# One key group's maximum subtracted on GpSimd, and a first tile stored from a copy, in a transformer block on one core

## The chip, the cores and the metric

The kernel runs on one core of a Trainium2 chip. The metric is device time of one execution in microseconds, the median of several runs. Five engines work side by side and are tied by semaphores only: TensorE (PE), VectorE (DVE), ScalarE (ACT), GpSimd (POOL) and SyncE (SP), which here issues the DMAs.

## The reference, cut to what matters

A block of a diffusion transformer over 2048 tokens and 256 context tokens of width 1024: modulated norm, projections, latent attention with 8 heads, a two-way retention with 8 heads, an output projection and a layer of 16 experts. The change touches the attention and the first tile of the projection.

```python
def block_attention(q, k, v):
    ...
    def one_block(qblk):
        s = jnp.einsum('bqhd,bkhd->bhqk', qblk, k).astype(jnp.float32) * scale
        p = jax.nn.softmax(s, axis=-1).astype(v.dtype)
        return jnp.einsum('bhqk,bkhd->bqhd', p, v)
...
    h = rmsnorm(x, g_norm_mix[layer]) * (1.0 + sc1) + sh1
    hc = rmsnorm(ctx, g_norm_mix[layer]) * (1.0 + csc1) + csh1
```

Each head has queries of width 96, 2048 of them, and 2304 keys. All is float32.

## The kernel before

The stages follow one another: projection (`project`), retention, attention (`attention`), output projection, experts.

**Attention** (lines 1220 to 1562) takes 32 blocks `b`, each one head and 512 queries. The keys are 18 tiles of 128 (`T`), in six groups of three (`GROUPS`, `G`). A block's scores stand with keys on the partitions and queries along the row, in one of two SBUF tiles `sc` of 18 x 512; blocks take them in turn. Every engine runs `turn(pair, j, b, more)` for each block; the order inside is written by hand, and an engine does its instructions in that order.

- TensorE (L1413): the scores of block b+1, tile by tile through four PSUM banks, each as three matmuls (`score`, L1368). After tile 11 come the probability sums of block b-1 (`prob_sum`, L1409), which need all of GpSimd's sums. Tile 12 may only overwrite its bank when VectorE's held maximum has read it. Then the weighted sum of block b in six groups (`weighted`, L1399). After group 2 it transposes the maxima of block b+1 (`max_rows`, L1380), after group 3 it spreads the column maxima over all partitions (`max_spread`, L1388: a matmul of a repeated column with the identity), into PSUM bank 4.
- ScalarE (L1470): exponential of group 0 (`probabilities`, L1462), nine score copies of b+1 out of PSUM (`copy_scores`, L1457), exponential of group 1, nine more copies, exponentials of groups 2 to 4, the finished output of b-1 (L1468), a part of the rounding of the next head's keys and queries (L1450), exponential of group 5.
- VectorE (L1547): subtraction of the maximum in groups 2 to 5 of block b (`shift`, L1545, which reads the spread maximum from PSUM); then the maximum over the keys of b+1: the held maximum (L1511) takes tiles 0, 1 from SBUF and 8, 9 from their PSUM banks, once tile 9 has been copied; six more pairs (L1518), the fold (L1525 to L1528), column maxima (`spread`, L1539), and the subtraction in groups 0 and 1 of b+1.
- GpSimd (L1343): a part of the splitting of the next head's keys and queries in six of eight blocks (`split`, L1341, two instructions), then five sums of the probabilities over the groups (L1349 once, L1353 four times), each after its exponential.
- SyncE stores each finished block and loads heads.

For the last block TensorE waits for GpSimd's sums and adds them (L1442).

**Projection.** For each of 18 token tiles VectorE makes `h_T_whole` (modulate, L649, L651), ScalarE rounds it (L547), VectorE forms the rest (`rest`, L659), and TensorE multiplies by the input weights (`z`, L410). The unrounded tile lies where the rest is written, so `rest` first waits until it is stored (`h_stored`). For tile 0 the store is issued by ScalarE (L604), for later ones by SyncE. ScalarE also rounds two parts of the input weights (L596) ahead of the statistics of tile 1. `kz` (`k_zeta`) is GpSimd's output of L616, first written in tile 0 after the retention keys are ready.

## Time and profile before

| | |
|---|---|
| median of 3 runs | 2913.35 us (2909.04 to 2915.96) |
| profiled execution | 2910.62 us, span 2908.8 us |
| busy over the span | PE 2607.9 us (90%), DVE 1975.1 (68%), ACT 1466.8 (50%), POOL 977.0 (34%) |
| 1100 to 1700 us, within attention | PE 536.89 of 600 us, DVE 486.45, ACT 456.85, POOL 450.29 |
| the same, granted TensorE clock | 1.00 |

Busy time tells how full an engine is, not what it waits for. For that the rows further down go through one block in order of time. In a timeline a row is a run of like instructions: start, time to its end, engine, line, operation, output<-input, shapes, count; in square brackets the idle time before it, and who ended it. Matmul ends are modelled, so the next start is the better mark of what a run costs. A float32 matmul is recorded as two or more instructions.

### The profile page before, as it was taken

The page shows a single profiled execution, that of the slowest core. Times are in us where ns is not written, and L with a number is a line of the kernel's source. Part 1 is how long each engine was busy: PE and PEld are TensorE (multiplying, and loading weights), DVE is VectorE, ACT ScalarE, POOL GpSimd, SP SyncE. Part 2 cuts the span into 40 slices and gives each one's busy share as a digit, 9 for nine tenths or more (in the row PEclk, how much of TensorE's full clock was granted, in tenths as well). Part 3 has the DMA queues.
Part 4 walks back from the last instruction along what each step waited for, and adds up shares of the span by engine and source line. Part 5 has one row for each costly group of instructions (what it writes and reads, how often), then busy time and mean ns, then how long its engine had stood idle before and what let it go on. Part 6 is the DMA issues. An engine that isn't in the chain of part 4 may idle for free. (4 is left out here: it accounts for less than half of the span.)

```text
span 2908.8 us, 44417 instructions
## 1 busy us (share of the span) xinstructions
PE 2607.9 (90%) x17109; PEld 2170.1 (75%) x17109; DVE 1975.1 (68%) x2885; ACT 1466.8 (50%) x2178; POOL 977.0 (34%) x578
## 2 busy tenths in 40 slices
PE   5999999899959898989889949992999999999996
PEld 3877877788846666666666628881999999999995
DVE  5555554777748887888788835557766767767666
ACT  4555554322237777877777732112344444444444
POOL 0111111222216777777777652220101101101112
PEclk7999999999969999999999979995999999999998
DMA  7644443322230110111010035434667767767678
GB/s 254 206 153 153 154 163 131 98 79 79 64 63 3 37 38 14 28 37 29 15 36 6 7 103 169 154 129 139 190 205 229 220 203 229 232 202 228 208 231 304
DMA packets 278856, 379.67 MB, mean 131 GB/s; under 512 B 36755, under 2 KB 200502, under 8 KB 276982
## 3 DMA queue, kind: packets, MB, share of 16 engines
q1 hardware_dynamic: 268998, 341.70, 36.9%
q0 software_dynamic: 9504, 34.61, 5.2%
q8 instruction: 137, 2.24, 0.3%
q14 instruction: 73, 0.60, 0.1%
q10 hardware_dynamic: 144, 0.52, 0.0%
HBM read 290.87 MB, written 85.90 MB: 130 GB/s over the span
## 5 line engine op out<-in xcount | busy, mean ns | idle before, releaser
L2143 PE MATMUL ebank<-gathered_T,w_gate_up 128*128 128x256 f32 x4608 | 546.5, 280 | 1.4 <-DVE gathered_T L2365 1.4
L2143 PEld LDWEIGHTS ebank<-gathered_T,w_gate_up 128*128 128x128 f32 x4608 | 543.2, 189 | 3.2 <-DVE gathered_T L2365 1.8
L1353 POOL TENSOR_TENSOR prob_sums<-prob_sums,scores 128x1536 f32<-128x1536 f32 x128 | 445.7, 3482 | 161.3 <-ACT scores L1462 147.4
L1545 DVE TENSOR_TENSOR scores<-scores,max_bank 128x1536 f32<-128x1536 f32 x192 | 322.4, 1748 | 59.3 <-PE max_bank L1388 59.3
L1462 ACT ACTIVATE scores<-scores 128x1536 f32<-128x1536 f32 x192 | 277.4, 1478 | 112.5 <-DVE scores L1545 112.5
L410 PE MATMUL bank<-w_in_sb,h_T 128*128 128x512 f32 (+1 forms) x1296 | 290.9, 383 | 12.1 <-DVE h_T L659 12.1
L1368 PE MATMUL score_banks<-head_qT,head_kT 96*128 96x512 f32 x960 | 254.3, 401 | 51.9 <-DVE max_bank L1511 33.9
L2157 PE MATMUL ebank<-w_down,hidden_T 128*128 128x512 f32 x1152 | 282.0, 400 | 3.1 <-DVE w_down L2375 2.9
L410 PEld LDWEIGHTS bank<-w_in_sb,h_T 128*128 128x128 f32 x1296 | 242.2, 189 | 46.5 <-DVE h_T L659 12.3
L1399 PE MATMUL abank<-scores,head_v 128*64 128x256 f32 x2304 | 270.3, 383 | 1.1 <-ACT scores L1462 0.9
L1368 PEld LDWEIGHTS score_banks<-head_qT,head_kT 96*128 96x128 f32 x960 | 177.6, 190 | 106.4 <-ACT scores L1457 42.6
L2076 POOL DMA_INDIRECT scratch_acc<-expert_out,slot_tokens x30 | 71.0, 2366 | 545.3 <-DVE expert_out L2394 540.8
L2157 PEld LDWEIGHTS ebank<-w_down,hidden_T 128*128 128x128 f32 x1152 | 213.8, 189 | 52.6 <-issue 4.8
L1518 DVE TENSOR_TENSOR max_bank<-scores,max_bank 128x1024 f32<-128x1024 f32 x192 | 236.0, 1229 | 20.4 <-ACT scores L1457 0.5
L1457 ACT ACTIVATE scores<-score_banks 128x512 f32<-128x512 f32 x320 | 190.7, 596 | 75.4 <-PE score_banks L1368 64.8
L1399 PEld LDWEIGHTS abank<-scores,head_v 128*64 128x64 f32 x2304 | 156.9, 137 | 91.8 <-issue 17.3
L2370 DVE TENSOR_TENSOR w_gate_up<-w_gate_up_whole,w_gate_up 128x2048 fp32r<-128x2048 f32 x96 | 215.4, 2285 | 13.5 <-ACT w_gate_up L2185 13.5
L1704 PE MATMUL obank<-w_o_sb,mix_tile 128*128 128x512 f32 x768 | 184.1, 396 | 26.8 <-POOL mix_tile L1679 26.8
L1368 PE MATMUL abank<-head_qT,head_kT 96*128 96x512 f32 x768 | 197.6, 393 | 0.0
L2185 ACT ACTIVATE w_gate_up<-w_gate_up_whole 128x2048 fp32r<-128x2048 f32 x96 | 178.2, 1905 | 37.3 <-DMA w_gate_up_whole<-in_w_exp_up 37.3
L2204 ACT ACTIVATE gate_exp<-ebank 128x256 f32<-128x256 f32 x96 | 36.8, 384 | 311.6 <-PE ebank L2143 311.6
L1704 PEld LDWEIGHTS obank<-w_o_sb,mix_tile 128*128 128x128 f32 x768 | 143.6, 190 | 56.0 <-POOL mix_tile L1679 27.2
(297 smaller groups left out, 4163.4 us busy)
## 6 DMA issues: line engine op xcount, KB each, us to landing
w_gate_up_whole<-in_w_exp_gate SPq DMA_DIRECT2D x48, 1024.0 KB, 5.9
w_gate_up_whole<-in_w_exp_up SPq DMA_DIRECT2D x48, 1024.0 KB, 8.8
w_down_whole<-in_w_exp_down SPq DMA_DIRECT2D x192, 256.0 KB, 5.8
ada_rest<-in_w_ada SPq DMA_DIRECT2D x16, 1024.0 KB
x_tile<-in_x_all SPq DMA_DIRECT2D x18, 512.0 KB
scratch_h<-h_T_whole SPq DMA_DIRECT2D x17, 512.0 KB, 2.7
ada_w<-in_w_ada SPq DMA_DIRECT2D x4, 2048.0 KB, 19.2
chunk_h_T_whole<-scratch_h SPq DMA_DIRECT2D x16, 512.0 KB
```

The source lines that it names most:

```text
L410: m = pe.matmul(banks[bank][:, 0:n], hT[u][:, hp, k, :], w_in[:, wp, k, lo:lo + n], start=(k == 0 and i == 0), stop=(k == KD - 1 and i == 2))
L1353: pool.tensor_tensor(a[:, :, :], a[:, :, :], p[:, g * G:(g + 1) * G, :], ALU.add).then_inc(sg["summed"].sem, 1)
L1368: m = pe.matmul(banks[S_BANKS[kt % 4]][:, :], kT[u][:, kp, k], qT[u][:, qp, q], start=(n == 0), stop=(n == 2))
L1399: m = pe.matmul(ps[64 * half:64 * half + 64, 0:HB], v1[u][:, kt, :], p[:, kt, half * HB:(half + 1) * HB], start=(kt == 0), stop=(kt == T - ...
L1457: act.activation(sc[j % 2][:, kt, :], banks[S_BANKS[kt % 4]][:, :], ACT.Copy).then_inc(sg["scores"].sem, 1)
L1462: act.activation(x, x, ACT.Exp, scale=ATT_SCALE).then_inc(sg["probs"].sem, 1)
L1518: dve.tensor_tensor(mx_psum[:, :, :], sc[j % 2][:, 2 * n:2 * n + 2, :], mx_psum[:, :, :], ALU.max).then_inc(sg["max_keys"].sem, 1)
L1545: dve.tensor_tensor(x, x, mid(banks[4], G), ALU.subtract).then_inc(sg["shifted"].sem, 1)
L1704: x = pe.matmul(banks[2 * u + half][:, :], mt[u][:, mp, k, :], w_o[:, wp, k, half * 512:(half + 1) * 512], start=(k == 0 and n == 0), stop ...
L2143: x = pe.matmul(banks[f % 3][:, j * CAP:(j + 1) * CAP], w_gu[c][:, wp, j, k, o:o + P], xsT[:, xp, k, :], start=(k == 0 and n == 0), stop=( ...
L2157: x = pe.matmul(banks[Y_BANKS[2 * c + h]][:, :], hid[:, hp, k, h * P:(h + 1) * P], w_d[i % RING][:, wp, :], start=(k == 0 and n == 0), sto ...
L2370: dve.tensor_tensor(w_gu[c][:, 1, j], w_gu_whole[c][:, 1, j], w_gu[c][:, 0, j].bitcast(F32), ALU.subtract).then_inc(sg["gu_rest"].sem, 1)
```

## The change

In attention, the subtraction of the maximum in group 5 (key tiles 15 to 17) goes from VectorE to GpSimd, which does it as the first instruction of its turn. GpSimd reads the maximum from a new SBUF tile `mx_all`. To fill it, TensorE spreads the maximum twice, into bank 4 and bank 3, with transposes in place of matmuls, and one key tile sooner: after two of the three tiles of group 3. ScalarE copies bank 3 to `mx_all` at the start of its turn. ScalarE copies ten score tiles, in place of nine, ahead of the exponential of group 1. In the last block GpSimd makes no sums and TensorE adds all 18 probability tiles; it takes the sums of block 30 after weighted group 0 in place of group 3. In the projection, GpSimd copies the first h tile into the still unused `kz`, and SyncE stores it from there; VectorE's `rest` of tile 0 waits for that copy and no longer for the store.

```diff
+            sp.wait_ge(h_kept, 2)
+            sp.dma_start(scratch["h"][0:P], kept).then_inc(sg["h_stored"].sem, 16)
...
-            sg["hT"].wait(act, 0)
-            act.dma_start(scratch["h"][0:P], hT_whole[0][:, 1, :, :]).then_inc(sg["h_stored"].sem, 16)
...
+                if t == 0:
+                    pool.wait_ge(h_kept, 3)
...
+            for g in range(2):
+                sg["hT"].wait(pool, 0, 2 * g + 2)
+                pool.tensor_copy(kept[:, 4 * g:4 * g + 4, :], hT_whole[0][:, 1, 4 * g:4 * g + 4, :]).then_inc(h_kept, 1)
...
-                sg["h_stored"].wait(dve, t)
+                if t:
+                    sg["h_stored"].wait(dve, t)
...
+                    if t == 0:
+                        dve.wait_ge(h_kept, g + 1)
...
             def turn(pair, j, b, more):
 
+                sg["max_kept"].wait(pool, b)
+                x = sc[j % 2][:, (GROUPS - 1) * G:, :]
+                pool.tensor_tensor(x, x, mid(mx_all[:, :], G), ALU.subtract).then_inc(sg["pool_shift"].sem, 1)
                 split_next(split, pair, j)
+                if not more:
+                    return
...
-                    m = pe.matmul(banks[4][:, c * P:(c + 1) * P], mq[:, c:c + 1].to_broadcast([P, P]), perm["ident"][:, :],
-                                  start=True, stop=True, skip_group_check=True)
+                    m = pe.transpose(banks[4][:, c * P:(c + 1) * P], mq[:, c:c + 1].to_broadcast([P, P]), perm["ident"][:, :])
                 m.then_inc(sg["max_psum"].sem, 1)
+                for c in range(4):
+                    m = pe.transpose(banks[3][:, c * P:(c + 1) * P], mq[:, c:c + 1].to_broadcast([P, P]), perm["ident"][:, :])
+                m.then_inc(sg["max_twice"].sem, 1)
...
-                    m = weighted(u, j, b, g)
-                    if more and g == 2:
+                    if more and g == 3:
                         max_rows(b + 1)
-                    if more and g == 3:
+                        weighted(u, j, b, g, range(2))
                         max_spread(b + 1)
-                    if not more and g == 3:
+                        m = weighted(u, j, b, g, range(2, G))
+                    else:
+                        m = weighted(u, j, b, g)
+                    if not more and g == 0:
                         prob_sum((j - 1) % 2, b - 1)
...
-            prob_sum((BLOCKS - 1) % 2, BLOCKS - 1)
+            ps, p = banks[5 + (BLOCKS - 1) % 2], sc[(BLOCKS - 1) % 2]
+            for kt in range(T):
+                for c in range(4):
+                    m = pe.matmul(ps[32 * c:32 * c + 32, HB:HB + P], ones[:, :], p[:, kt, c * P:(c + 1) * P],
+                                  start=False, stop=(kt == T - 1), skip_group_check=True)
+            m.then_inc(sg["out_psum"].sem, 1)
...
+            def keep_max(b):
+                sg["max_twice"].wait(act, b)
+                sg["pool_shift"].wait(act, b - 1)
+                act.activation(mx_all[:, :], banks[3], ACT.Copy).then_inc(sg["max_kept"].sem, 1)
...
             def turn(pair, j, b, more):
+                keep_max(b)
                 probabilities(j, b, 0)
                 if more:
                     sg["valued"].wait(act, b - 1)
-                    for g in range(3):
-                        copy_scores((j + 1) % 2, b + 1, g)
+                    copy_scores((j + 1) % 2, b + 1, 0, HELD + 2)
                 probabilities(j, b, 1)
                 if more:
-                    for g in range(3, GROUPS):
-                        copy_scores((j + 1) % 2, b + 1, g)
+                    copy_scores((j + 1) % 2, b + 1, HELD + 2, T)
...
-                sg["max_psum"].wait(dve, b - 1)
+                sg["max_kept"].wait(dve, b - 1)
...
-                for g in range(2, GROUPS):
+                for g in range(2, GROUPS - 1):
                     shift(j, b, g)
```

The first tile's `kz` also has to wait for its store: SyncE raises `h_kept` to 3 once the store has landed, after it has issued the store of the retention keys.

## Rows read from the trace of the kernel before

**Rows 1.** The head of the page.
```profile
span 2908.8 us, 44417 instructions
```

**Rows 2.** Waits, 874 to 1717 us: engine and line, releaser, us in total, times, longest.
```profile
DVE max_bank L1511 <- ACT scores L1457: 45.7, 31, 1.5
...
PE max_bank L1380 <- DVE score_max L1528: 50.5, 30, 2.0
...
PE score_banks L1368 <- DVE max_bank L1511: 33.9, 31, 1.9
```

**Rows 3.** Timeline of PE over one block: start, length, instructions, idle before.
```profile
1217.19 1.66 PE L1368 MATMUL score_banks<-head_qT,head_kT 96*128 96x512 f32 x6
...
1225.58 0.86 PE L1409 MATMUL abank<-prob_sums,ones 128*32 128x128 f32 x24
1227.51 1.61 PE L1368 MATMUL score_banks<-head_qT,head_kT 96*128 96x512 f32 x6 [1.07 <-DVE max_bank L1511]
...
1231.76 4.11 PE L1399 MATMUL abank<-scores,head_v 128*64 128x256 f32 x36
1237.54 0.66 PE L1380 MATMUL max_bank<-ident,score_max 128*128 128x128 f32 x4 [1.67 <-DVE score_max L1528]
1238.12 1.52 PE L1399 MATMUL abank<-scores,head_v 128*64 128x256 f32 x12
1239.57 1.16 PE L1388 MATMUL max_bank<-ident,max_cols 128*128 128x128 f32 x8
1240.66 2.81 PE L1399 MATMUL abank<-scores,head_v 128*64 128x256 f32 x24
1243.40 1.67 PE L1368 MATMUL score_banks<-head_qT,head_kT 96*128 96x512 f32 x6
```

**Rows 4.** Timeline of DVE over the same block.
```profile
1226.13 1.23 DVE L1511 TENSOR_TENSOR max_bank<-scores,score_banks 128x1024 f32<-128x1024 f32 x1 [1.50 <-ACT scores L1457]
...
1236.80 0.69 DVE L1528 TENSOR_TENSOR score_max<-score_max,max_bank 128x512 f32<-128x512 f32 x1
1238.23 0.69 DVE L1539 TENSOR_REDUCE max_cols<-max_bank 128x4 f32<-128x512 f32 x1 [0.75 <-PE max_bank L1380]
1240.77 10.07 DVE L1545 TENSOR_TENSOR scores<-scores,max_bank 128x1536 f32<-128x1536 f32 x6 [1.84 <-PE max_bank L1388]
```

**Rows 5.** Timeline of ACT over the same block.
```profile
1223.64 0.60 ACT L1457 ACTIVATE scores<-score_banks 128x512 f32<-128x512 f32 x1
1224.14 1.48 ACT L1462 ACTIVATE scores<-scores 128x1536 f32<-128x1536 f32 x1
1225.52 0.58 ACT L1457 ACTIVATE scores<-score_banks 128x512 f32<-128x512 f32 x1
```

**Rows 6.** Timeline of POOL over the same block.
```profile
1233.92 14.37 POOL L1353 TENSOR_TENSOR prob_sums<-prob_sums,scores 128x1536 f32<-128x1536 f32 x4 [4.75 <-ACT scores L1462]
```

**Rows 7.** Groups of POOL by shape: busy us, mean ns, idle before.
```profile
L1349 POOL TENSOR_TENSOR prob_sums<-scores 128x1536 f32<-128x1536 f32 x32 | 111.3, 3477 | 55.5 <-ACT scores L1462 55.5
...
L616 POOL TENSOR_TENSOR k_zeta<-ret_k_rows,zeta 128x512 f32<-128x512 f32 x36 | 44.5, 1255 | 337.6 <-DVE ret_k_rows L671 337.6
L1341 POOL TENSOR_TENSOR head_kT<-head_kT_whole,head_kT 96x768 fp32r<-96x768 f32 x21 | 39.0, 1856 | 33.4 <-ACT head_kT L1450 33.4
```

**Rows 8.** Timelines of DVE and PE at the end of attention.
```profile
1683.01 0.69 DVE L1528 TENSOR_TENSOR score_max<-score_max,max_bank 128x512 f32<-128x512 f32 x1
...
1712.20 1.51 PE L1409 MATMUL abank<-prob_sums,ones 128*32 128x128 f32 x24 [11.85 <-POOL prob_sums L1353]
```

**Rows 9.** Timelines of DVE, PE and ACT at the opening.
```profile
54.05 1.29 DVE L659 TENSOR_TENSOR h_T<-h_T_whole,h_T 128x512 fp32r<-128x512 f32 x2 [6.38 <-DMA scratch_h<-h_T_whole]
...
55.39 11.85 PE L410 MATMUL bank<-w_in_sb,h_T 128*128 128x416 f32 x48 [11.54 <-DVE h_T L659]
...
61.76 0.52 ACT L554 ACTIVATE z_latent<-bank 128x416 f32<-128x416 f32 x1 [2.26 <-PE bank L410]
```

**Rows 10.** Line 1545 alone: ns min/median/max, first and last start us.
```profile
L1545 DVE TENSOR_TENSOR scores<-scores,max_bank x192: 1744/1747/1756, 874.7 to 1695.3; 128x1536 f32<-128x1536 f32 x192
```

More of the change, by code:

```diff
@@ L216, in project @@
         zero_state = sem("zero_state")
+        h_kept = sem("first_h_kept")
+        kept = kz[:, :, :, :].rearrange("p h w d -> p (h w d)").rearrange("p (k n) -> p k n", k=KD)
         w_rounded = sem("w_in_rounded")
@@ L366, in turn @@
                 store(t, "ret_k", rk[:, :], scratch["rk"][at, :], "rk_stored")
+                if t0 == 0:
+                    sg["h_stored"].wait(sp, 0)
+                    sp.sem_inc(h_kept, 1)
                 if ahead:
@@ L1244, in attention @@
         mx = sb("score_max", [P, QB])
+        mx_all = sb("max_spread", [P, QB])
         mq = sb("max_cols", [P, 4])
@@ L1387, in max_spread, with weighted @@
                 for c in range(4):
-                    m = pe.matmul(banks[4][:, c * P:(c + 1) * P], mq[:, c:c + 1].to_broadcast([P, P]), perm["ident"][:, :],
-                                  start=True, stop=True, skip_group_check=True)
+                    m = pe.transpose(banks[4][:, c * P:(c + 1) * P], mq[:, c:c + 1].to_broadcast([P, P]), perm["ident"][:, :])
                 m.then_inc(sg["max_psum"].sem, 1)
-            def weighted(u, j, b, g):
+                for c in range(4):
+                    m = pe.transpose(banks[3][:, c * P:(c + 1) * P], mq[:, c:c + 1].to_broadcast([P, P]), perm["ident"][:, :])
+                m.then_inc(sg["max_twice"].sem, 1)
+            def weighted(u, j, b, g, part=range(G)):
                 ps, p = banks[5 + j % 2], sc[j % 2]
@@ L1396, in weighted @@
                 sg["probs"].wait(pe, b, g + 1)
-                for kt in range(g * G, (g + 1) * G):
+                for kt in (g * G + t for t in part):
                     for half in range(2):
@@ L1450, in split, with copy_scores @@
                     act.activation(x[:, 0, c], whole[:, 1, c], ACT.Copy).then_inc(sg["rounded"].sem, 1)
-            def copy_scores(j, b, g):
-                sg["summed"].wait(act, b - 2, max(g, 1))
-                for kt in range(g * G, (g + 1) * G):
+            def copy_scores(j, b, first, end):
+                for kt in range(first, end):
+                    if kt % G == 0:
+                        sg["summed"].wait(act, b - 2, max(kt // G, 1))
                     sg["s_psum"].wait(act, b, kt + 1)
                     act.activation(sc[j % 2][:, kt, :], banks[S_BANKS[kt % 4]][:, :], ACT.Copy).then_inc(sg["scores"].sem, 1)
+            def keep_max(b):
+                sg["max_twice"].wait(act, b)
+                sg["pool_shift"].wait(act, b - 1)
+                act.activation(mx_all[:, :], banks[3], ACT.Copy).then_inc(sg["max_kept"].sem, 1)
             def probabilities(j, b, g):
                 x = sc[j % 2][:, g * G:(g + 1) * G, :]
-                sg["shifted"].wait(act, b, g + 1)
+                if g < GROUPS - 1:
+                    sg["shifted"].wait(act, b, g + 1)
+                else:
+                    sg["pool_shift"].wait(act, b)
                 act.activation(x, x, ACT.Exp, scale=ATT_SCALE).then_inc(sg["probs"].sem, 1)
@@ L1492, in _ @@
                 split(0, 0, n)
-            for g in range(GROUPS):
-                copy_scores(0, 0, g)
+            copy_scores(0, 0, 0, T)
             split(1, 1, 0)
```

5 lines of the change are left out of this document (3 added, 2 removed).

## Prediction

> **What bounds the kernel now.** I read the page first: the profiled execution spans 2908.8 us [rows 1], and attention, from about 874 to 1714 us, is the only stretch that the edit reaches over and over (32 blocks). Then I read the list of waits over that stretch, then one block on each engine in order of time. The waits name two stops of TensorE that recur in every block: it waits for the held maximum (33.9 us in 31 times) and for the folded maximum (50.5 us in 30 times). The held maximum on VectorE waits in its turn for a score copy of ScalarE, 45.7 us in 31 times, 1.5 us each [rows 2].
>
> One block shows how the three hang together. Let S be the moment at which TensorE begins the scores of the next block. S is 1217.19, the next one is 1243.40, so the period is 26.21 us [rows 3]. Scores of twelve key tiles and the 24 records of the probability sums end at 1225.58 + 0.86 = S+9.25; TensorE waits 1.07 us; scores of the last six tiles run from 1227.51 to 1231.76 (4.25); three groups of the weighted sum take 4.11; it waits 1.67 us; then four transposes (0.58 to the next start), one weighted group, the spreading and two more groups, 5.86 us from 1237.54 to the next S [rows 3]. The two waits are 2.74 us; 23.47 us are work.
>
> VectorE begins the held maximum H at 1226.13 = S+8.94 and ends the fold F at 1236.80 + 0.69 = 1237.49 = H+11.36, with nothing idle between; TensorE begins the transposes 0.05 us later [rows 3, 4]. So the period is the sum (S to H) 8.94 + (H to F) 11.36 + 0.05 + 5.86 = 26.21 us. VectorE is not what delays H: its six subtractions end at 1240.77 + 10.07 = 1250.84, 1.5 us before the next H would come. H waits for the copy of key tile 9. ScalarE copies tile 8 at 1223.64, then puts the exponential of group 1 (1.48 us) in front, and copies tile 9 only at 1225.52, up to 1226.10 [rows 5].
>
> **The change in attention.** (a) The copy order. Ten tiles are now copied before the exponential of group 1. Tile 9 follows tile 8 at TensorE's pace, twelve tiles in 8.39 us or 0.70 us each [rows 3]: copy 9 runs from about 1224.34 to 1224.92, and H comes at S+7.76 instead of S+8.94, 1.18 us sooner. The exponential of group 1 then ends near S+9.1 and the copies of tiles 10 and 11 near S+10.3. They are wanted by the maximum of the sixth pair at H+5.3 = S+13, and by the scores of tile 14 at S+10.6, so this part costs nothing; the cover is 0.3 us at tile 14.
>
> (b) One subtraction of six leaves VectorE, 10.07/6 = 1.68 us. VectorE was waiting for the copy at that point, so this buys nothing by itself. It keeps (a) from running into a new wait: with six subtractions VectorE would be free at about the new S+6.4, with five at S+4.7, both before S+7.76.
>
> (c) TensorE. The held maximum ends at S+9.0 and the sums at S+9.25, so the wait of 1.07 us goes. TensorE reaches the transposes after 9.25 + 4.25 + 4.11 = S+17.61, and the fold now ends at 7.76 + 11.36 = S+19.12: what is late next is the same fold, with a wait of 1.56 us in the place of 1.67. The spreading was four plain matmuls, 8 records, 1.09 us to the next start; it becomes four transposes, whose price stands in the transposes of the maximum, 0.58 us [rows 3], and these are issued twice: 1.16, so +0.07. It also moves one key tile forward. It would start 0.58 + 0.97 (8 of 12 records of 1.45 us) after the transposes began, F+1.60; the column maxima, which it needs, are ready 1.43 us after F (1238.23 + 0.69) [rows 4]. That leaves 0.17 us of cover. VectorE can start to subtract at about F+2.3 instead of F+3.28, ScalarE's first exponential ends before the next S, and its score copies wait for TensorE, as they do now.
>
> (d) ScalarE gets one copy of 128x512 from PSUM, 0.60 us by a score copy [rows 5]. It waits for the second spreading (F+2.9) and lies ahead of the exponential of group 0, which waits for VectorE until F+4.1. It is done at F+3.5, so it is hidden. If it were not, up to 0.6 us per block would shift the exponential, which has 1.1 us before the first score copy.
>
> (e) GpSimd. It does five sums a block, four of them in 14.37 us [rows 6], 3.58 from one to the next, and two weight splits of 1.86 us in three blocks of four [rows 7]. The subtraction is not in the trace. Nearest is the two-operand add of the same shape, 3.48 us; a multiply by a repeated operand takes 1.26 us for 512 columns, which times three is 3.77 us [rows 7]. Below 3.48 I see no row; the bounds are 3.4 and 3.8 and I take 3.58 with its gap, since the shape is the same. The load of a block with splits is 6 x 3.58 + 3.7 = 25.2 us, against a new period of 25.1: just full. Without splits it is 21.5. The four adds begin when the exponential of group 2 is done, S+15.65 (now 1233.92 = S+16.73), and end at the next S+4.9; subtraction to S+8.5, splits to S+12.2, first add to S+15.7. Who waits for this: the probability sums on TensorE at S+8.4, 3.5 us of slack; the exponential of group 5 at S+20.4, 12 us of slack; ScalarE's copies into the old score tile, more. A drift of 0.1 us a block is given back in each fourth block.
>
> The new period is 7.76 + 11.36 + 0.05 + 5.86 + 0.07 = 25.10 us, 1.11 less. 31 blocks have the next block's scores beside them: 34.4 us.
>
> **The end of attention.** The fold of the last block ends at 1683.01 + 0.69 = 1683.70. Now TensorE waits 11.85 us for GpSimd's last sum and ends at 1712.20 + 1.51 = 1713.71, F+30.0 [rows 8]. In the new kernel GpSimd does no sums of block 31. It ends those of block 30 at F+10.9 (1233.92 + 14.37 stands at F+10.8 of its block [rows 4, 6]); TensorE, which now asks for them right after group 0, adds them by F+11.8, then does four weighted groups by F+17.3, the fifth by F+18.7 (GpSimd's subtraction ends at F+14.5, its exponential at F+16). Then come 72 sum matmuls in the place of 12: 6 x 0.86 = 5.2 us, F+23.8. Gain 6.2 us. TensorE stood idle for 11.85 us before its records took 1.51 instead of 0.86 us; if its clock is low after the 3.5 us stop too, up to 3.5 us are lost; if not, nothing. I take nothing and keep 3.5 for the range.
>
> **The opening.** VectorE waited 6.38 us, from 47.67 to 54.05, until the first hidden tile was stored, and TensorE began its first product at 55.39 [rows 9]. Now VectorE waits for a GpSimd copy. No row shows a GpSimd copy; by the 1.26 us of its multiply of 512 columns [rows 7] the second half is kept at 48.9 and subtracted by 49.6, so TensorE starts some 5.7 us sooner. What is late next is ScalarE: it stood 2.26 us before the latent copy at 61.76, so it is free for it at 59.50 [rows 9], held up by the weight rounding and the statistics of the next tile, which the edit doesn't move. The latent chain hence gains 2.26 us only and TensorE will wait for it. I take 2.3, with 1 and 5.5 as ends. The store goes to SyncE's queue, behind its loads and ahead of the load of the third x tile. That load is wanted some 29 us later. GpSimd's first k_zeta must wait for the store, which lands long before.
>
> **Sum.** 34.4 + 6.2 + 2.3 = 42.9 us. Against the profiled execution's 2910.62 us this gives 2867.7; that one ran 2.73 us below the median of the runs, 2913.35, so on the median 2870.4.
>
> **A rule that speaks against the move.** GpSimd and VectorE both work through the stretch, and the VectorE subtraction took 1744 to 1756 ns in all 192 cases, beside a GpSimd add or not [rows 10]. The Trainium skill, "Perfetto Trace Analysis", section Optimizing Scalar/DVE Operations, warns that offloading between VectorE and GpSimd might not help, since they share an SBUF read port. This case's trace does not bear the warning out so far for this form, whose second operand is in PSUM; rival 1 is what it would mean here.
>
> **Rivals.** (1) The two engines hold each other up after all. GpSimd's subtraction runs from S+4.9 to S+8.5; if VectorE may not start in it, H moves from S+7.76 to S+8.5 and the block gains 0.37 us: 31 x 0.37 + 8.5 = 20 us, 2893. Against it stand the even durations of rows 10. Chance 5%.
>
> (2) The held maximum does not come sooner, because the wait for the kept maximum or the copies' pace takes the place of the exponential. Then the block keeps 26.2 us and the ends alone gain 8.5: 2905. Half of it is as possible: TensorE's 0.17 us of cover is gone or tile 14 waits, 0.3 us a block, 2880; that half lies within my range. Chance of the full case 4%.
>
> (3) GpSimd becomes the bound and the kernel is slower. Mean load is 5 x 3.58 + 0.75 x 3.7 + x = 20.7 + x, so beyond x = 5.5 us for the subtraction the period exceeds the present 26.2. At twice the add, 7.0 us, it is 27.7, 1.5 us more in each of 31 blocks, +46 - 8.5 = +38 us, 2951. For it: GpSimd is full to 0.1 us in blocks with splits. Against it: rows 7 bound x by 3.8. Chance 5%.
>
> (4) More is gained: TensorE without any wait would have a period of 23.5 us, but the fold chain forbids it. The opening at its upper end and a first block that ran at the low clock could give 4 us more. That lies in the range.
>
> **How the numbers follow.** Forecast 2870, chance 84% with the small variants; rivals 5, 4, 5%, 2% for anything else. The range goes from 2860 (opening 3.2 more, noise of the runs, 0.2 us a block more) to 2886 (tail clock 3.5, opening 1.3, 0.35 us a block less). A difference under 0.2%, 5.8 us, can't be told from no change; faster by more than that 93%, within it 2%, slower 5%.
>
> **What would show it.** In the trace after: period near 25.1; no wait of TensorE for the held maximum and about 1.5 us for the fold; VectorE idle near 3 us ahead of the held maximum, still released by a score copy; GpSimd's subtraction near 3.5 us and no idle in blocks with splits; at the end a TensorE wait of 3.5 us for sums and 144 records. A period above 25.5, or a TensorE wait for prob_sums within the blocks, would prove the reckoning wrong.

## The result and the profile after

The median is 2865.11 us (4 runs, 2864.64 to 2872.16) beside 2912.84 us for the kernel before in the same job: a ratio of 0.984, 95% interval 0.982 to 0.986. The forecast was 2870 us, with a range of 2860 to 2886. The profiled execution took 2864.79 us; its head, where [rows 1] has 2908.8 us:

```profile
span 2862.8 us, 44715 instructions
...
PE 2607.9 (91%) x17229; PEld 2170.4 (76%) x17229; DVE 1921.4 (67%) x2853; ACT 1490.4 (52%) x2210; POOL 1072.7 (37%) x607
```

TensorE is busy for the same 2607.9 us as before, and the span is 46.0 us shorter, so the waits are the place to look. The list of waits of the kernel after, 866 to 1680 us (who waited, for whom, us in total, times, longest), where [rows 2] has three entries:

```profile
DVE max_bank L1546 <- ACT scores L1486: 90.3, 31, 4.0
...
PE max_bank L1399 <- DVE score_max L1563: 57.8, 32, 6.0
```

VectorE waits twice as long as before for a score copy, 90.3 in place of 45.7 us. TensorE still waits for the fold, 57.8 in place of 50.5 us; 6.0 of the 57.8 are the wait of the first block, which lies ahead of the window of [rows 2]. What is missing is TensorE's wait of 33.9 us for the held maximum: one of 0.7 us is left of the 31. One block on TensorE (start, length, instructions, idle before), to be laid beside [rows 3]:

```profile
1201.20 1.66 PE L1387 MATMUL score_banks<-head_qT,head_kT 96*128 96x512 f32 x6
...
1209.61 0.86 PE L1430 MATMUL abank<-prob_sums,ones 128*32 128x128 f32 x24
1210.42 1.63 PE L1387 MATMUL score_banks<-head_qT,head_kT 96*128 96x512 f32 x6
...
1214.71 4.11 PE L1420 MATMUL abank<-scores,head_v 128*64 128x256 f32 x36
1220.45 0.66 PE L1399 MATMUL max_bank<-ident,score_max 128*128 128x128 f32 x4 [1.64 <-DVE score_max L1563]
...
1222.05 0.65 PE L1407 MATMUL max_bank<-ident,max_cols 128*128 128x128 f32 x4
1222.54 0.60 PE L1410 MATMUL max_bank<-ident,max_cols 128*128 128x128 f32 x4
1223.07 3.24 PE L1420 MATMUL abank<-scores,head_v 128*64 128x256 f32 x28
1226.24 1.66 PE L1387 MATMUL score_banks<-head_qT,head_kT 96*128 96x512 f32 x6
```

The same block on VectorE, beside [rows 4]:

```profile
1209.05 1.23 DVE L1546 TENSOR_TENSOR max_bank<-scores,score_banks 128x1024 f32<-128x1024 f32 x1 [2.93 <-ACT scores L1486]
...
1219.71 0.69 DVE L1563 TENSOR_TENSOR score_max<-score_max,max_bank 128x512 f32<-128x512 f32 x1
...
1222.74 8.41 DVE L1580 TENSOR_TENSOR scores<-scores,max_bank 128x1536 f32<-128x1536 f32 x5 [0.90 <-PE max_bank L1407]
```

The period is 1226.24 - 1201.20 = 25.04 us, where it was 26.21. The held maximum H begins at S+7.85 (S+8.94 before); the fold ends at 1220.40, H+11.35; 0.05 us later TensorE transposes; from there to the next S it is 5.79 us (5.86 before). H still waits for a score copy, only for one that comes 1.1 us sooner. The transposes of the spreading cost a little less than those of the maximum (0.59 us to the next start): 0.49 and 0.53 us, for two spreadings, where one spreading by matmuls took 1.09 us [rows 3].

GpSimd over the same time, in a block that has both splits:

```profile
1206.18 3.51 POOL L1361 TENSOR_TENSOR scores<-scores,max_spread 128x1536 f32<-128x1536 f32 x1
1209.63 1.86 POOL L1355 TENSOR_TENSOR head_kT<-head_kT_whole,head_kT 96x768 fp32r<-96x768 f32 x1
1211.44 1.86 POOL L1355 TENSOR_TENSOR head_qT<-head_qT_whole,head_qT 96x768 fp32r<-96x768 f32 x1
1213.25 3.50 POOL L1368 TENSOR_TENSOR prob_sums<-scores 128x1536 f32<-128x1536 f32 x1
1216.89 14.34 POOL L1372 TENSOR_TENSOR prob_sums<-prob_sums,scores 128x1536 f32<-128x1536 f32 x4
```

No row has a bracket: GpSimd stands idle nowhere in this block, and the subtraction costs as much as an add. The block before this one, with splits too, has one gap of 0.16 us, the block after it one of 0.67. ScalarE's copy of the maximum (0.60 us at 1223.18) is hidden, since ScalarE still waits 0.76 us for VectorE ahead of the next exponential:

```profile
1224.53 1.48 ACT L1499 ACTIVATE scores<-scores 128x1536 f32<-128x1536 f32 x1 [0.76 <-DVE scores L1580]
```

The end of attention on TensorE, beside [rows 8]:

```profile
1658.98 0.86 PE L1430 MATMUL abank<-prob_sums,ones 128*32 128x128 f32 x24 [3.54 <-POOL prob_sums L1372]
1659.77 6.70 PE L1420 MATMUL abank<-scores,head_v 128*64 128x256 f32 x60
1666.40 4.14 PE L1468 MATMUL abank<-scores,ones 128*32 128x128 f32 x144
```

The last fold ended at 1648.16, so the sums are done at F+22.4 (F+30.0 before), 1670.54 in place of 1713.71.

The whole span, place by place: first score matmul 849.13 before, 847.5 after (-1.6 us); from there to the last fold 834.6 and 800.7 (-33.9); the end -7.6. That is 43.2 us at the end of attention. The other 2.8 us arise in the stages behind it, which the edit leaves as they are.

The blocks are not all alike. Nearly all periods after are 25.0 us, but two are 26.95 and 27.01. In both TensorE waited 1.99 us for the fold, and right behind that its granted clock was 0.50 for 3.4 us (the row of such a stretch: busy us and instructions of PE, PEld, DVE, ACT and POOL, then the clock):

```profile
995.12:998.53 3.41, 3.41 (x18) 2.37 (x18) 2.12 (x2) 1.37 (x3) 3.27 (x2) 0.50 0.02 5
```

A third block with a wait of 1.99 us kept the full clock and took 25.37 us, so the half clock cost 1.6 us in each of the two, 3.2 us of the blocks' gain in this execution. The kernel before has no such stretch between 892 and 1704 us.

### The profile page after: what moved, and what is told of

It reads as the page before. It is cut to its first block and busy times, and to the rows that moved or that the text cites. A ratio compares the mean times of both kernels' runs of the same rounds, so it can differ in the third digit from the quotient of the medians.

```text
span 2862.8 us, 44715 instructions
## 1 busy us (share of the span) xinstructions
PE 2607.9 (91%) x17229; PEld 2170.4 (76%) x17229; DVE 1921.4 (67%) x2853; ACT 1490.4 (52%) x2210; POOL 1072.7 (37%) x607
## 5 line engine op out<-in xcount | busy, mean ns | idle before, releaser
L1372 POOL TENSOR_TENSOR prob_sums<-prob_sums,scores 128x1536 f32<-128x1536 f32 x124 | 431.8, 3483 | 56.3 <-ACT scores L1499 41.0
L1580 DVE TENSOR_TENSOR scores<-scores,max_bank 128x1536 f32<-128x1536 f32 x160 | 269.2, 1749 | 30.9 <-PE max_bank L1407 30.9
```

Of the source, the lines that this page charges most:

```text
L1372: pool.tensor_tensor(a[:, :, :], a[:, :, :], p[:, g * G:(g + 1) * G, :], ALU.add).then_inc(sg["summed"].sem, 1)
L1580: dve.tensor_tensor(x, x, mid(banks[4], G), ALU.subtract).then_inc(sg["shifted"].sem, 1)
```

## The experiments

The theory after this reading: the copy order gives nearly all of it, some 31 us, and moving the subtraction gives nothing itself. The first rival: the move to GpSimd is what brings the block forward. The second: the opening and the end hold a good part.

### The opening alone

The projection of the kernel after with the attention of the kernel before.

```diff
-            act.dma_start(scratch["h"][0:P], hT_whole[0][:, 1, :, :]).then_inc(sg["h_stored"].sem, 16)
+            sp.dma_start(scratch["h"][0:P], kept).then_inc(sg["h_stored"].sem, 16)
```

> The kernel before with the opening of the change alone: GpSimd's copy of the first h tile and the store from it by SyncE; attention as before. My step says 2.3 us less than before (the latent chain moves by ScalarE's 2.26 us), with 1 and 5.5 us as ends. Rival, from the trace after: TensorE begins 8 us earlier but gives it back at a low granted clock and at the next tile's store, and the first modulation sum stood only 0.7 us earlier: 0 to 1 us. Second rival: the whole 5.7 us of the earlier first product stays.

Measured: 2910.34 beside 2912.54 us, ratio 0.9993 (0.9984 to 1.0002). That is 2.2 us less, which can't be told from nothing. TensorE at this kernel's opening:

```profile
49.47 6.08 PE L417 MATMUL bank<-w_in_sb,h_T 128*128 128x416 f32 x24 [5.66 <-DVE h_T L672]
...
65.21 0.55 PE L442 MATMUL bank<-ident,latent_normed 128*128 128x128 f32 x3 [2.10 <-DVE latent_normed L724]
...
65.63 7.36 PE L417 MATMUL bank<-w_in_sb,h_T 128*128 128x512 f32 x24
```

The first product starts 5.9 us sooner than the 55.39 of [rows 9]. What follows gives most of it back: TensorE stops 2.10 us for the latent, and the next product of 24 records takes 7.36 us, where the one just ahead of it (56.46) takes 5.78; the granted clock was 0.50 from 65.96 to 69.37 us, and the same product in the kernel before took 5.78. What follows this product starts at 72.83, 1.1 us sooner than before (73.92).

### The copy order alone

The kernel before, with ten copies in place of nine ahead of the exponential of group 1, and nothing else. (The wait for the old score tile moves into the loop over the tiles, since ten is not a whole number of groups.)

```diff
-                    for g in range(3):
-                        copy_scores((j + 1) % 2, b + 1, g)
+                    copy_scores((j + 1) % 2, b + 1, 0, HELD + 2)
```

> The kernel before with the copy order alone: ten score tiles ahead of the exponential of group 1. No GpSimd subtraction, one spreading at its old place. My theory (the copy of tile 9 sets the held maximum, VectorE's subtraction doesn't): VectorE's six subtractions end 13.35 us after the fold, which is S+7.4 of the new period, the held maximum comes at S+7.85, period 7.85 + 11.36 + 0.05 + 5.86 = 25.1, 1.1 us less in 31 blocks, 34 us less than before. Rival (GpSimd's help is what brings the gain): VectorE is late without it and the gain is under 5 us.

Measured: 2881.27 us, ratio 0.9893 (0.9876 to 0.9911), 31.3 us less than before. The period is 1232.88 - 1207.78 = 25.10 us. TensorE's two starts and VectorE in this kernel:

```profile
1207.78 1.66 PE L1368 MATMUL score_banks<-head_qT,head_kT 96*128 96x512 f32 x6
...
1232.88 1.43 PE L1368 MATMUL score_banks<-head_qT,head_kT 96*128 96x512 f32 x5
```

```profile
1205.15 10.07 DVE L1543 TENSOR_TENSOR scores<-scores,max_bank 128x1536 f32<-128x1536 f32 x6 [1.84 <-PE max_bank L1388]
1215.61 1.23 DVE L1509 TENSOR_TENSOR max_bank<-scores,score_banks 128x1024 f32<-128x1024 f32 x1 [0.38 <-ACT scores L1458]
```

With all six subtractions on VectorE it still stands idle for 0.38 us before H, which begins at S+7.83. So the engine was not short of time for the earlier H, and the move of the subtraction was not needed for it. Two thirds of the whole gain is this one line.

### All but GpSimd's subtraction

The kernel after, with the subtraction of group 5 back on VectorE, the maximum spread once (by transposes, one tile sooner) and no copy of it on ScalarE.

```diff
-                x = sc[j % 2][:, (GROUPS - 1) * G:, :]
-                pool.tensor_tensor(x, x, mid(mx_all[:, :], G), ALU.subtract).then_inc(sg["pool_shift"].sem, 1)
...
-                keep_max(b)
...
-                for g in range(2, GROUPS - 1):
+                for g in range(2, GROUPS):
                     shift(j, b, g)
```

> The changed kernel with the subtraction of group 5 back on VectorE, one early spreading by transposes, no copy of the maximum by ScalarE. Copy order, end and opening as in the changed kernel. My theory (the move to GpSimd buys nothing and costs TensorE the second spreading): VectorE is free at S+7.0, before the held maximum at S+7.85; TensorE saves four transposes, 0.53 us a block, period 24.5, about 16 us less than the changed kernel, 63 less than before. Rival (the move pays): VectorE becomes late by up to its 1.68 us and the kernel is up to 50 us slower than the changed one.

Measured: 2854.17 us, ratio 0.9806 (0.9791 to 0.9821), 10.9 us less than the kernel after, and the two intervals don't meet. TensorE's two starts, with the transposes of the maximum between them, and VectorE in this kernel:

```profile
1219.86 1.66 PE L1383 MATMUL score_banks<-head_qT,head_kT 96*128 96x512 f32 x6
...
1239.09 0.66 PE L1395 MATMUL max_bank<-ident,score_max 128*128 128x128 f32 x4 [1.64 <-DVE score_max L1547]
...
1244.44 1.67 PE L1383 MATMUL score_banks<-head_qT,head_kT 96*128 96x512 f32 x6
```

```profile
1216.80 10.08 DVE L1564 TENSOR_TENSOR scores<-scores,max_bank 128x1536 f32<-128x1536 f32 x6 [0.90 <-PE max_bank L1403]
1227.69 1.23 DVE L1530 TENSOR_TENSOR max_bank<-scores,score_banks 128x1024 f32<-128x1024 f32 x1 [0.81 <-ACT scores L1479]
```

H is at S+7.83 here and at S+7.85 in the kernel after: five subtractions or six, it is the same moment. From the transposes to the next S it is 5.35 us in place of 5.79, since the second spreading is gone; 31 x 0.44 = 13.6 us. At the end of attention the two traces are 15.6 us apart, with 3.2 us for the two stretches at half clock, of which this kernel's blocks have none; the stages behind take 2.6 us longer in this trace. The two spans differ by 13.0 us, the two medians by 10.9. The move that the change is named after, with the second spreading that it needs, costs the kernel 11 us, of which by the traces some 3 may be the clock's.

One more piece can be read here. With one spreading, moved a tile forward and done by transposes, it is 5.35 us from the transposes of the maximum to the next S; with one spreading by matmuls, in the kernel before and in the one with the copy order alone, it is 5.86. By this 0.51 us in 31 blocks, some 16 us is an estimate of what the new form of the spreading gains, and the second spreading takes 13.6 of them back. No run has the transposes alone.

### The change with the old copy order

The kernel after, with nine copies first.

```diff
-                    copy_scores((j + 1) % 2, b + 1, 0, HELD + 2)
+                    copy_scores((j + 1) % 2, b + 1, 0, HELD + 1)
...
-                    copy_scores((j + 1) % 2, b + 1, HELD + 2, T)
+                    copy_scores((j + 1) % 2, b + 1, HELD + 1, T)
```

> The changed kernel with nine score copies ahead of the exponential of group 1, as before; all else as changed. My theory: the held maximum goes back to S+8.9, TensorE's wait of about 1 us for it returns, period near 26.1, 34 us more than the changed kernel (about 2899). Rival (the shorter VectorE work carries the gain): within 5 us of the changed kernel.

Measured: 2901.28 us, ratio 0.9963 (0.9948 to 0.9978), 36 us more than the kernel after. The period is 26.15 us. VectorE and, behind it, TensorE:

```profile
1222.51 1.23 DVE L1546 TENSOR_TENSOR max_bank<-scores,score_banks 128x1024 f32<-128x1024 f32 x1 [4.05 <-ACT scores L1486]
```

```profile
1223.88 1.63 PE L1387 MATMUL score_banks<-head_qT,head_kT 96*128 96x512 f32 x6 [1.07 <-DVE max_bank L1546]
```

VectorE has been relieved of a subtraction and only stands idle for it, 4.05 in place of 1.50 us [rows 4]; H is at S+8.96, and TensorE's wait of 1.07 us is back to the hundredth. The first rival is refuted from both sides.

### The end alone

The kernel before, with GpSimd making no sums of the last block, the sums of block 30 asked for after group 0, and 72 sum matmuls.

```diff
+                if not more:
+                    return
...
-                    if not more and g == 3:
+                    if not more and g == 0:
...
-            prob_sum((BLOCKS - 1) % 2, BLOCKS - 1)
+            for kt in range(T):
+                for c in range(4):
+                    m = pe.matmul(ps[32 * c:32 * c + 32, HB:HB + P], ones[:, :], p[:, kt, c * P:(c + 1) * P], ...)
```

> The kernel before with the end of the change alone: in the last block TensorE adds the 18 probability tiles and GpSimd makes no sums. My step said 6.2 us less; the trace after (72 matmuls in 4.14 us in the place of my 5.2) says about 7.5 us, here a little more, since GpSimd has no subtraction at the end: 7 to 9 us less than before, 2904 to 2906. Rival: TensorE's clock falls after its stop of 3.5 us and the gain is 3 us.

Measured: 2906.14 beside 2912.61 us, ratio 0.9979 (0.9970 to 0.9988), 6.5 us less. TensorE at the end:

```profile
1702.07 1.51 PE L1411 MATMUL abank<-prob_sums,ones 128*32 128x128 f32 x24 [2.56 <-POOL prob_sums L1355]
1703.51 7.45 PE L1401 MATMUL abank<-scores,head_v 128*64 128x256 f32 x60
```

Here, after a stop of 2.56 us, the 24 records took 1.51 us and the 60 records of the weighted sum 7.45. In the kernel after it was 0.86 and 6.70 us, after a longer stop. In this trace the sums are done at F+23.7, 6.3 us sooner than before; the 1.4 us are about what that lacks of the kernel after's 7.6. (The profiled execution is the slowest of the eleven, 2912.74 us; its first score matmul comes at 855.1 us, 6 us later than in the kernel before, so it lost its time ahead of attention, not here.)

How the clock stands at this place is not fixed by the code. The kernel with the old copy order has the same instructions here as the kernel after, and the same stop to 0.01 us:

```profile
1691.42 1.51 PE L1430 MATMUL abank<-prob_sums,ones 128*32 128x128 f32 x24 [3.53 <-POOL prob_sums L1372]
```

Its 60 records take 8.96 us in place of 6.70, the granted clock being 0.50 from 1690.65 to 1697.48 us, and the sums are done at F+25.3 in place of F+22.4.

### GpSimd with two groups

The kernel after, with groups 4 and 5 subtracted on GpSimd. It prices rival 3.

```diff
-                x = sc[j % 2][:, (GROUPS - 1) * G:, :]
-                pool.tensor_tensor(x, x, mid(mx_all[:, :], G), ALU.subtract).then_inc(sg["pool_shift"].sem, 1)
+                for g in (GROUPS - 2, GROUPS - 1):
+                    x = sc[j % 2][:, g * G:(g + 1) * G, :]
+                    pool.tensor_tensor(x, x, mid(mx_all[:, :], G), ALU.subtract).then_inc(sg["pool_shift"].sem, 1)
```

> The changed kernel with GpSimd subtracting in groups 4 and 5, VectorE in four groups. It prices GpSimd's load. Reckoning of rival 3: 7 x 3.58 + 0.75 x 3.7 = 27.8 us mean load against the period of 25.04, so GpSimd becomes the bound, 2.8 us more in each of 31 blocks, +85 us on the changed kernel, near 2950, slower than before. Rival: GpSimd's sums have enough slack towards TensorE and the period grows by less than 1 us.

Measured: 2929.49 us, ratio 1.0058 (1.0045 to 1.0072), slower than the kernel before and 64 us more than the kernel after. TensorE:

```profile
1233.34 1.51 PE L1431 MATMUL abank<-prob_sums,ones 128*32 128x128 f32 x24 [4.17 <-POOL prob_sums L1373]
1234.77 2.93 PE L1388 MATMUL score_banks<-head_qT,head_kT 96*128 96x512 f32 x6
```

GpSimd is the bound now and TensorE waits for its sums, 66.0 us in 25 times. The periods are uneven, 25.0 us in half of the blocks and up to 32.0 in the others, 26.9 on average where 27.8 was reckoned. Six score records take 2.93 us behind the stop in place of 1.63. Since one group more makes the kernel slower than before, the one group that was moved used up nearly all that GpSimd had.

### The held maximum four tiles sooner, with and without GpSimd's subtraction

If the first maximum is the wait that ends last, it should take tiles 4 and 5 from PSUM. Then H can start four tiles sooner, but only if VectorE is free by then. Both kernels make ten copies first; the sums of the block before are still taken after tile 11.

```diff
-    HELD = 8
+    HELD = 4
...
-                        if kt == HELD + 3 and has_before(pair, j):
+                        if kt == 11 and has_before(pair, j):
```

First on the kernel after:

> The changed kernel with the held maximum over tiles 0, 1 and 4, 5 in the place of 8, 9 (probability sums still after tile 11, ten copies ahead of the exponential). The held maximum then waits for VectorE and not for a copy, so here GpSimd's help should be worth something: VectorE is free at S+4.9, H = S+5.1, tile 8 stops 0.9 us for its bank, the fold is ready before TensorE. TensorE's own work gives a period of 24.3, GpSimd's load (21.5 plus 3.7 in three of four blocks) 24.3: 0.7 us less in 31 blocks, 21 us less than the changed kernel, near 2844. Rival (GpSimd is already too full): no gain.

Measured: 2843.51 us, ratio 0.9760 (0.9746 to 0.9773), 21.6 us less than the kernel after. TensorE and VectorE:

```profile
1190.24 1.66 PE L1387 MATMUL score_banks<-head_qT,head_kT 96*128 96x512 f32 x6
...
1196.68 1.61 PE L1387 MATMUL score_banks<-head_qT,head_kT 96*128 96x512 f32 x6 [0.68 <-ACT scores L1486]
```

```profile
1219.59 1.23 DVE L1546 TENSOR_TENSOR max_bank<-scores,score_banks 128x1024 f32<-128x1024 f32 x1 [0.15 <-ACT scores L1486]
```

The S before this H is at 1214.52, so H is at S+5.07. Within the blocks TensorE no longer waits for the fold (once, 3.3 us, at the start of attention); what is late next is a score copy, 0.68 us, and the period is 1214.52 - 1190.24 = 24.28.

Then on the kernel without GpSimd's subtraction:

> The kernel of e3_no_gpsimd (all six subtractions on VectorE, one spreading) with the held maximum over tiles 0, 1 and 4, 5, as in e8_held_early. The pair of this one and e8_held_early shows what GpSimd's subtraction is worth where the held maximum waits for VectorE. My theory: VectorE is free at S+7.0 only, tile 8 can't overwrite its bank before S+8.4 and TensorE stops 2.8 us there, period 17.6 + 2.8 + 5.35 = 25.8, 1.2 us more than e3_no_gpsimd in 31 blocks, near 2892, 48 us more than e8_held_early. Rival (the subtraction's place never matters): within 5 us of e8_held_early.

Measured: 2970.40 beside 2913.47 us, ratio 1.0206 (1.0192 to 1.0220). The expectation was missed by 78 us. TensorE:

```profile
1240.07 1.66 PE L1383 MATMUL score_banks<-head_qT,head_kT 96*128 96x512 f32 x6
...
1248.44 2.90 PE L1383 MATMUL score_banks<-head_qT,head_kT 96*128 96x512 f32 x6 [2.64 <-DVE max_bank L1530]
1251.14 2.76 PE L1383 MATMUL abank<-head_qT,head_kT 96*128 96x512 f32 x6
```

The wait is the one that the theory named: VectorE begins H at S+7.0, straight from its sixth subtraction, and TensorE may not go on with tile 8 until VectorE has read the held banks. Its price was not foreseen. Six records behind the stop take 2.76 us, 1.52 at full speed; the granted clock from 1100 to 1600 us is 0.90 here and 1.00 in the kernel before:

```profile
1100.00:1600.00 500.00, 451.25 (x2756) 313.22 (x2755) 375.47 (x299) 357.36 (x467) 352.85 (x116) 0.90 0.11 25
```

This period is 29.03 us; nearly all lie between 27.5 and 29.1, 28.2 on average, where 25.8 was expected. The pair of runs shows that the same edit, GpSimd's subtraction, costs 11 us in one order and is worth 127 us in another: it pays where VectorE is the engine that H waits for. Of the 127 us some 48 were expected from the stop itself. The rest goes with the low clock behind it: in the block shown the twelve records take 2.6 us more than at full clock, and the sums behind them 0.4.

### A first maximum that needs no held bank

The kernel without GpSimd's subtraction, whose first maximum takes tiles 0 to 3 from SBUF. It waits for four copies in place of ten, and TensorE doesn't wait for it.

```diff
-                sg["scores"].wait(dve, b, HELD + 2)
+                sg["scores"].wait(dve, b, 4)
...
-                dve.tensor_tensor(mx_psum[:, :, :], sc[j % 2][:, 0:2, :], held[:, :, :], ALU.max)...
+                dve.tensor_tensor(mx_psum[:, :, :], sc[j % 2][:, 0:2, :], sc[j % 2][:, 2:4, :], ALU.max)...
```

> The kernel of e3_no_gpsimd, with the first maximum over tiles 0 to 3, all from SBUF, and no held banks: VectorE may begin it as soon as tile 3 is copied, TensorE's tile 12 waits for nothing. VectorE is free at S+7.0 in e3_no_gpsimd and waited 0.8 us for tile 9, so my theory gives a period of 24.58 - 0.8 = 23.8, 31 times, 25 us less than e3_no_gpsimd. Rival: this is the one VectorE instruction of the loop with two SBUF inputs, and GpSimd works at that time in blocks with splits. The Trainium skill, SBUF - State Buffer, says that such an instruction contends with a GpSimd instruction that reads SBUF and one of them blocks. In rows: the opening's GpSimd copy took 1.01 beside a VectorE subtraction of two SBUF inputs and 0.61 us without. If VectorE waits for GpSimd's running instruction, up to 1.9 us at a split, the gain shrinks to under 10 us.

Measured: 2840.82 us, ratio 0.9752 (0.9739 to 0.9765), 13.4 us less than with the held banks: between the two expectations. Line 1528 alone (ns min/median/max, first and last start), and one of the long ones on VectorE:

```profile
L1528 DVE TENSOR_TENSOR max_bank<-scores x32: 1232/1242/1954, 854.0 to 1606.3; 128x1024 f32<-128x1024 f32 x32
```

```profile
1218.98 1.90 DVE L1528 TENSOR_TENSOR max_bank<-scores 128x1024 f32<-128x1024 f32 x1
```

The instruction now has both inputs in SBUF, and it lies beside GpSimd's splitting of the next head, which lengthens too. GpSimd by line and shape (busy us, mean ns):

```profile
L1354 POOL TENSOR_TENSOR head_qT<-head_qT_whole,head_qT 96x768 fp32r<-96x768 f32 x13 | 35.9, 2762 | 0.0
```

2762 ns in place of 1854. Two periods in a row, counted from H to H, are 23.91 and 24.58 us; the longer one has the long maximum at its start.

### The same, with the splitting out of the way

The kernel of the last section, with the splits behind GpSimd's first add of the block.

```diff
-                split_next(split, pair, j)
                 if not more:
                     return
...
                 pool.tensor_tensor(..., p[:, G:2 * G, :], ALU.add).then_inc(sg["summed"].sem, 1)
+                split_next(split, pair, j)
```

> The kernel of e5_pairs_from_sbuf with GpSimd's two weight splits behind its first sum, away from the VectorE instruction with two SBUF inputs. In e5_pairs_from_sbuf that instruction took up to 1.90 in the place of 1.23 us, and the split beside it 2.8 in the place of 1.85 us; blocks without a split had a period of 23.9, with one up to 24.6. My theory (contention with the split): all blocks come to about 23.9, 0.3 us a block less on average, 8 us less than e5_pairs_from_sbuf, near 2833, the fastest of all. Rival: the splits now delay the sums, the sums end next to the same instruction, and nothing is gained.

Measured: 2830.51 us, ratio 0.9718 (0.9705 to 0.9731), 10.3 us less than the kernel before it and 34.6 less than the kernel after. It is the fastest of all, and it leaves the subtraction on VectorE. Line 1528 alone:

```profile
L1528 DVE TENSOR_TENSOR max_bank<-scores x32: 1232/1234/1234, 853.4 to 1596.9; 128x1024 f32<-128x1024 f32 x32
```

All 32 now take 1.23 us, and the period is 23.91 in nearly every block; from the first H to the last it is 8.8 us less than in the last kernel, and the thirteen lengthened maxima there had cost some 8.6 us. So the collision was what the last kernel lacked. The Trainium skill, "SBUF — State Buffer", section Who interferes with whom, says that a VectorE instruction with two SBUF inputs contends with a GpSimd instruction that reads SBUF, and one with at most one SBUF input does not. Both halves agree with the rows here: 1.23 against up to 1.95 us for the one, and 1746 to 1756 ns in all 160 subtractions of the kernel after for the other.

At this point VectorE itself sets the block: six subtractions 10.07, maxima 11.36, and 2.35 us from the end of the fold to the first subtraction, with the gap of 0.13 between, are 23.91. Whether a group on GpSimd would pay there was not tried. GpSimd's mean load would be 5 x 3.58 + 3.51 + 2.4 = 23.8 us (the splits of the kernel after take 74.0 us in 31 blocks, 2.4 each, since every third query split is only 512 columns wide): as full as the period, so it leaves little room. That is an estimate and settles nothing.

## Why the prediction was right

**The copy order.** Predicted: copy 9 comes sooner, H at S+7.76, 1.18 us per block. Measured S+7.85, 1.09. The copy order alone gives 31.3 us of the 47.7, and the kernel after without it has a period of 26.15. Shown by both runs.

**VectorE's relief buys nothing.** Predicted that too, but with the remark that it keeps the earlier H from a new wait. The remark's own figures (VectorE free at S+6.4 with six; S+7.0 measured) already showed it was not needed, and the runs say the same: VectorE is idle for 0.38 us ahead of H with six subtractions. The prediction did not draw the conclusion, that the kernel would be faster without the move.

**TensorE.** The wait for the held maximum gone, the wait for the fold 1.56 predicted and 1.64 measured. From the transposes to the next S: 5.93 predicted, 5.79 measured. The two spreadings take 0.49 and 0.53 us, not 0.58 each. The cover of 0.17 us for moving the spreading a tile forward held: one wait of 0.8 us in 32 stands before it. The period of 25.10 came out as 25.04. The prediction called the two spreadings +0.07 us and so did not see that one of them by itself would have been worth 0.5 us a block.

**GpSimd and ScalarE.** Subtraction 3.51 us, bounds 3.4 and 3.8, taken 3.58 with its gap; next to no idle in the blocks with splits that were looked at (none, 0.16 and 0.67 us); TensorE's probability sums wait for nothing within the blocks, and once at the end. The copy of the maximum is hidden.

**The end.** 6.2 us predicted, 7.6 measured. The stop of 3.54 us is the one predicted (3.5), and the clock stayed full. That was luck: the prediction put the tail clock at nothing and kept 3.5 us for the range, and in the kernel with the old copy order the same stop was followed by half clock and the sums ended 2.9 us later after the fold. The term that was mis-sized is the 72 sum matmuls: six times 0.86 us were taken, 5.2 us, and they took 4.14. Why six short runs in a row cost less than six times one was not tested. Measured alone the end is worth 6.5 us.

**The opening.** 2.3 us predicted, with ends of 1 and 5.5. The steps are right as far as the latent: TensorE starts 5.9 us sooner in the kernel with the opening alone, and ScalarE's latent copy lies at 59.38, predicted 59.50. Behind it the prediction had nothing more, and there the product at half clock took 1.6 us back. The size can't be confirmed: 2.2 us is within the noise of that measurement. The traces point the same way without fixing it: the nine with the new opening reach the first score matmul at 846.5 to 849.6 us, the three with the old one at 849.1, 851.2 and 855.1. In the profiled execution of the kernel after, the first hidden tile was also ready 2.6 us sooner (45.02, before 47.66): a load landed 1.1 us sooner, and 16 records ahead of it took 1.92 us in place of 3.52. This is not the edit's doing, for in the kernel with the opening alone the tile is ready at 47.61.

**The sum.** 34.4 + 6.2 + 2.3 = 42.9 us were expected, and at the end of attention 43.2 stand: 33.9 within the blocks, 7.6 at the end, 1.6 ahead of attention. That the 33.9 meets the forecast's 34.4 so well is in part luck, two errors against each other: the shorter period alone would have given some 37 us, and the two stretches at half clock, for which the prediction had no term, took 3.2. The median came out 4.9 us under the forecast. 2.8 us of it arose in later stages, and no run says why. Most of the rest is the 2.73 us that the forecast added for the distance of the profiled execution from the median: after, that distance was 0.3 us.

**The rivals.** Rival 1, the two engines in each other's way, did not occur: all 160 subtractions of VectorE kept their 1.75 us. It exists in this kernel for another form, two SBUF inputs, where it cost about 9 us. Rival 2, something else in the exponential's place, did not occur. Rival 3, GpSimd as the bound, would have been the true danger: with one group more the kernel is slower than before, ratio 1.006. Its load was reckoned nearly right: full in blocks with splits, though a little lower on average, since every third query split is short.

## What to carry to other kernels

Find the wait that ends last before an engine is relieved: here the engine stood idle for another's copy, and one copy ahead of one exponential was worth 31 us, the move of 1.7 us of work a block minus 11. The same move was worth 127 us once the order of the block had made VectorE the engine waited for, so an offload should be tried again after each change of order. What an offload adds on the critical engine (a second spreading, 0.44 us in 31 blocks) is paid at once, whatever it frees. And where a change has several parts, one of them can hide another: here the cheaper form of the spreading covered the price of doing it twice.

## What the runs showed of the hardware

**TensorE's clock after short stops.** Stops of 2.64 to 2.79 us in nearly every block brought score matmuls to about half speed for some 5 us (six records 2.76 us, 1.52 at full), and so did one of 4.17 us. Stops of 1.64 us left the clock at full. Between these the same stop goes either way. Of three stops of 1.99 us in the kernel after, those that ended at 993.62 and 1270.84 us were followed by a granted clock of 0.50 for 3.4 us, the one that ended at 1397.95 was not. The stop of 3.54 us at the end of attention left the clock at 1.00 in the kernel after and in the one without GpSimd's subtraction; one of 3.53 us ahead of the same instructions was followed by 0.50 in the kernel with the old copy order. The length of the stop alone doesn't decide, and what does was not settled.

**Two engines in SBUF.** In the kernel whose first maximum reads SBUF alone, the instruction that began first kept its time, and the one that began second grew by a little less than the time in which both were under way. One such place, beside VectorE's maximum of 1.90 us at 1218.98:

```profile
1217.93 1.86 POOL L1354 TENSOR_TENSOR head_kT<-head_kT_whole,head_kT 96x768 fp32r<-96x768 f32 x1
1219.74 2.29 POOL L1354 TENSOR_TENSOR head_qT<-head_qT_whole,head_qT 96x512 fp32r<-96x512 f32 x1
```

The key split was under way and kept its 1.86 us; the maximum, which shared 0.81 us with it, took 0.67 us more than its 1.23; the query split, which began during the maximum and shared 1.15 us with it, took 2.29 us in place of 1.29. Where the key split had only 0.15 us left (1195.07), the maximum took 1.24 us. All nineteen maxima with splits beside them follow this, so who starts first decides who pays.

**A copy on GpSimd.** 512 columns took 0.61 us, half of its two-input operations of that size (1.26 us [rows 7]); one of the two took 1.01 us, and in that one's time VectorE subtracted with two SBUF inputs (line 672, from 44.94 to 45.63, its usual 0.69 us):

```profile
43.76 0.61 POOL L641 COPY k_zeta<-h_T_whole 128x512 f32<-128x512 f32 x1 [43.33 <-DVE h_T_whole L661]
45.08 1.01 POOL L641 COPY k_zeta<-h_T_whole 128x512 f32<-128x512 f32 x1 [0.72 <-DVE h_T_whole L661]
```
